# The stored sample states enter the product with q as plain float32, in four column tiles of TensorE

## The reference

```
def retention_chunk(q, k, v, S):
    ...
    scores = jnp.einsum('bhld,bhmd->bhlm', q, k) * dmask
    out = (jnp.einsum('bhlm,bhmv->bhlv', scores, v)
           + jnp.einsum('bhld,bhdv->bhlv', q, S) * q_decay[:, :, None])
    S_new = S * s_decay[:, None, None] + jnp.einsum('bhmd,bhmv->bhdv', k * k_decay[:, :, None], v)
    return out, S_new
```

## Time and profile before

| | |
|---|---|
| median of 3 runs | 1718.25 us (1717.4 to 1718.27) |
| the profiled execution | 1717.73 us |
| its span, first to last instruction | 1716.2 us |
| PE busy | 1691.2 us (99%) |
| DVE busy | 1109.4 us (65%) |
| ACT busy | 670.4 us (39%) |
| mean granted TensorE clock | 0.997 of 2.4 GHz |

### The profile page before, as it was taken

The page is one execution under the profiler, slowest core; times in us unless marked ns, Lnnn a source line. Parts: engine busy times, 40 slices in busy tenths (PEclk is TensorE's granted clock), DMA queues, the critical chain, the costliest instruction groups (busy, mean ns, idle before and its releaser), DMA issues.

```text
span 1716.2 us, 30964 instructions
## 1 busy us (share of the span) xinstructions
PE 1691.2 (99%) x11054; PEld 1642.6 (96%) x11054; DVE 1109.4 (65%) x1700; ACT 670.4 (39%) x982; POOL 172.1 (10%) x239
## 2 busy tenths in 40 slices
PE   7999999999999999999999999999999999999996
PEld 7999999999999999999999999999999999999995
DVE  6656657656656665765675665787776666666465
ACT  4533433443343343343243334453333333333333
POOL 1000000100100100000010010340000000000243
PEclk9999999999999999999999999999999999999998
DMA  8547846865764774784785586444754444444442
GB/s 329 183 149 250 286 149 226 299 185 172 283 234 155 280 270 155 258 280 137 259 292 169 184 287 217 142 138 139 243 197 147 147 147 147 147 147 150 148 147 98
DMA packets 101657, 342.04 MB, mean 199 GB/s; under 512 B 13680, under 2 KB 18416, under 8 KB 101568
## 3 DMA queue, kind: packets, MB, share of 16 engines
q1 hardware_dynamic: 81216, 265.49, 46.2%
q0 software_dynamic: 20352, 75.24, 12.9%
HBM read 292.30 MB, written 40.52 MB: 194 GB/s over the span
## 4 chain that ended last, share of the span: by engine, by line
PE 97%; ACT 1%; DVE 1%; DMA 0%; SPq 0%; issue 0%; POOL 0%; ACTq 0%; DVEq 0%; POOLq 0%
PE proj L1274 24%; PE proj L1279 24%; PE proj L1275 24%; PE proj L1420 4%; PE proj L1428 4%; PE proj L1421 4%; PE qs L1384 2%; PE qs L1385 2%; PE side L1265 1%; PE side L1260 1%; PE side L1259 1%; PE side L1258 1%; PE side L1296 1%; PE qs L1258 0%; PE qs L1259 0%; PE qs L1260 0%
## 5 line engine op out<-in xcount | busy, mean ns | idle before, releaser
L1274 PE MATMUL proj<-x_hi,w_hi 128*128 128x322 f32 (+2 forms) x2528 | 768.0, 314 | 8.2 <-DVE x_lo L796 7.9
L1275 PE MATMUL proj<-x_lo,w_hi 128*128 128x322 f32 (+2 forms) x2528 | 764.5, 313 | 0.0
L526 ACT CAST w_hi<-w_raw 128x1024 fp32r<-128x1024 f32 x416 | 435.6, 1049 | 429.7 <-PE proj L1275 238.9
L786 DVE TENSOR_TENSOR w_lo<-w_raw,w_hi 128x1024 fp32r<-128x1024 f32 x416 | 513.6, 1238 | 82.8 <-ACT w_hi L526 61.3
L1274 PEld LDWEIGHTS proj<-x_hi,w_hi 128*128 128x128 f32 x2528 | 477.8, 189 | 18.2 <-issue 12.2
L1275 PEld LDWEIGHTS proj<-x_lo,w_hi 128*128 128x128 f32 x2528 | 477.1, 189 | 4.2
L1279 PE MATMUL proj<-x_hi,w_lo 128*128 128x322 f32 (+2 forms) x2528 | 431.3, 313 | 0.7 <-DVE w_lo L786 0.7
L1279 PEld LDWEIGHTS proj<-x_hi,w_lo 128*128 128x128 f32 x2528 | 391.8, 189 | 1.2 <-DVE w_lo L786 1.2
L1420 PE MATMUL proj<-qk_or_z,w_hi 128*128 128x322 f32 x480 | 146.3, 315 | 0.2
L1421 PE MATMUL proj<-qk_or_z,w_hi 128*128 128x322 f32 x480 | 144.0, 311 | 0.0
L877 DVE TENSOR_TENSOR s_lo<-te_for_q_or_prompt_state,s_hi 128x512 fp32r<-128x512 f32 x128 | 85.9, 688 | 85.7 <-ACT s_hi L563 85.6
(11 more groups left out here) (190 smaller groups left out, 1442.7 us busy)
## 6 DMA issues: line engine op xcount, KB each, us to landing
w_raw<-w_head SPq DMA_DIRECT2D x256, 512.0 KB, 4.2
w_raw<-w_conv SPq DMA_DIRECT2D x128, 512.0 KB, 3.5
state_update<-s_in POOLq DMA_DIRECT2D x64, 512.0 KB, 7.3
te_for_q_or_prompt_state<-s_in SPq DMA_DIRECT2D x64, 512.0 KB, 5.2
s_out<-state_update POOLq DMA_DIRECT2D x64, 512.0 KB, 5.5
w_raw<-w_cout SPq DMA_DIRECT2D x32, 512.0 KB, 3.6
s_prompt<-te_for_q_or_prompt_state POOLq DMA_DIRECT2D x8, 512.0 KB, 3.6
head_table<-tables POOLq DMA_DIRECT2D x8, 441.0 KB, 5.0
```

Source lines behind the costliest of these rows:

```text
L526: act.copy(w_hi[:, i % SPL, :], w_raw[:, i % RAW, :]).then_inc(w_h.sem, 1)
L786: TT(w_lo[:, i % SPL, :], w_raw[:, i % RAW, :], f(w_hi[:, i % SPL, :]), ALU.subtract).then_inc(w_l.sem, 1)
L1274: mm(bank[:, 0:n], wh[:, k, :], rhs_h(k), start=(first and k == 0), stop=False)
L1275: x = mm(bank[:, 0:n], wh[:, k, :], rhs_l(k), start=False, stop=False)
```

## The change

- A state is no longer split. TensorE reads it from `sa` as plain float32, and q, multiplied with its decay by VectorE, stands in `qz` as plain float32 too.
- A matmul now has 32 stationary columns: 8 of them hold q of one sample, 24 are zero. It writes 32 partitions of the bank, which are one column tile of the array. Samples of even number and the key halves 0 and 1 take the tiles at 0 and 32, samples of odd number those at 64 and 96. `QP_AT` puts four groups of four such matmuls (two samples by two key halves) behind the chunks 6, 8, 12 and 15 of a head. Each is written as one matmul of 32 columns by 512.
- `s_round`, `s_rest`, their buffers and their semaphores go. So do the split of q for this product and ScalarE's copy into `qz`. VectorE writes `qz` with four small multiplications in place of one and two subtractions.
- `sa` has four buffers. The state loads stand at the chunks 5 to 8 and 11 to 14, those of the samples 4 to 7 wait for the group of the same head that frees their buffer (`state_pairs_used`), and the wait for the prompt's state moves from sample 0 to sample 3.
- The matrix of the fold has its ones in other rows; the fold is otherwise the same.

```
-QS_AT = {5: (0,), 6: (1,), 7: (2,), 10: (3, 4), 11: (5,), 12: (6, 7), 13: (8,), 14: (9, 10), 15: (11,),
-         16: (12, 13), 17: (14,), 18: (15,)}
+QP_AT = {6: 0, 8: 1, 12: 2, 15: 3}
-SA_AT = {5: 0, 7: 1, 12: 2, 14: 3, 16: 4, 17: 5, 18: 6, 20: 7}
+SA_AT = {5: 0, 6: 1, 7: 2, 8: 3, 11: 4, 12: 5, 13: 6, 14: 7}
...
-        qz = rb("q_spread", [DKB, NB * 136], F32R)
+        qz = rb("q_spread", [DKB, NB // 2 * 72])
-        sa = rb("state_for_q_or_prompt_state", [2, DKB, DV])
-        s_hi, s_lo = rb("s_hi", [2, DV], F32R), rb("s_lo", [2, DV], F32R)
+        sa = rb("state_for_q_or_prompt_state", [4, DKB, DV])
...
 (SyncE)
-                        sp.wait_ge(s_l.sem, s_l.at(h, 2 * b - 2))
-                        if b == 0:
+                        sp.wait_ge(s_q.sem, s_q.at(h, b // 2 - 1))
+                        if b == 3:
                             sp.sem_inc(passed.sem, 1)
                             sp.wait_ge(st_free.sem, st_free.at(h, 0))
-                        sp.dma_start(sa[:, b % 2, :, :], s_in[b, h]).then_inc(sa_in[b % 2].sem, 16)
+                        sp.dma_start(sa[:, b % 4, :, :], s_in[b, h]).then_inc(sa_in[b % 4].sem, 16)
...
 (ScalarE)
-                    act.copy(s_hi[:, t % 2, :], sa[:, b % 2, t % 2, :]).then_inc(s_h.sem, 1)
...
 (VectorE)
-                    TT(s_lo[:, t % 2, :], sa[:, b % 2, t % 2, :], f(s_hi[:, t % 2, :]), ALU.subtract).then_inc(s_l.sem, 1)
...
+                        for d in range(DKB):
+                            qd = by_pair(q_raw[:, d, NP_:N])
+                            for e in range(2):
+                                z = TT(qz_rows[e][:, d], qd[:, :, e], dec[:, :, e], ALU.mult)
+                        z.then_inc(qz_set.sem, 1)
...
 (TensorE)
-                        qb = qz[:, d, P * b:P * b + P]
-                        mm(bank_q[:, :], qb, s_hi[:, t % 2, :], start=(t == 0), stop=False)
-                        x = mm(bank_q[:, :], qb, s_lo[:, t % 2, :], start=False, stop=(t == 15))
+                        for e in range(2):
+                            b = 2 * q + e
+                            pe.wait_ge(sa_in[b % 4].sem, sa_in[b % 4].at(h, 16 * (b // 4 + 1)))
+                            for d in range(DKB):
+                                rows = slice(64 * e + 32 * d, 64 * e + 32 * d + 32)
+                                x = mm(bank_q[rows, :], qz[:, d, 32 * b:32 * b + 32], sa[:, b % 4, d, :],
+                                       start=(q == 0), stop=(q == NB // 2 - 1))
                         x.then_inc(s_q.sem, 1)
```

More of the change, by code:

```diff
@@ L192, in hybrid_step @@
         y_n = vt_yn[:, :].rearrange("p (t n) -> p t n", t=3)
-        pst = sa[:, 0]
-        qz_rows = qz[:, :, :].rearrange("p k (b c) -> p k b c", c=136)
+        pst = sa[:, 3]
+        qz_rows = [qz[:, :, :].rearrange("p k (q c) -> p k q c", c=72)[:, :, :, 32 * e:32 * e + DSEQ] for e in range(2)]
         ret.close()
@@ L230, in hybrid_step @@
         q_t, q_rot, q_h, q_l = count("q_temp"), count("q_rotated", 2), count("q_hi_made"), count("q_lo_made")
-        qs_t, qz_h, qz_l = count("q_decayed"), count("q_spread_hi"), count("q_spread_lo")
+        qz_set = count("q_spread_set")
         k_t, k_rot, k_h, k_l = count("k_temp"), count("k_rotated", 2), count("k_hi_made"), count("k_lo_made")
@@ L239, in hybrid_step @@
         vt_done, vn_h, vn_l = count("v_turned", 3), count("v_rows_hi", 3), count("v_rows_lo", 3)
[L240 to L243, removed]
+        sa_in = [count(f"state_q_in{i}", 32) for i in range(4)]
+        s_q = count("state_pairs_used", NB // 2, 1)
         yf_h, yf_l = count("y_fold_hi"), count("y_fold_lo")
@@ L384, in _ @@
             pool.memzero(a_lo[:, :].bitcast(F32))
-            pool.memzero(qz[:, :, :].bitcast(F32))
+            pool.memzero(qz[:, :, :])
             pool.memzero(k_ps[:, :].bitcast(F32))
@@ L578, in side @@
                         act.copy(q_hi, q_raw).then_inc(q_h.sem, 1)
[L579 to L582, removed]
                     if i == 8:
@@ L616, in side @@
                     if i == 19:
-                        act.wait_ge(s_q.sem, s_q.at(h, 2 * NB))
+                        act.wait_ge(s_q.sem, s_q.at(h, NB // 2))
                         act.copy(y_f[:, 0, :], bank_q[:, :]).then_inc(yf_h.sem, 1)
@@ L636, in head @@
                     side(i)
-                    for t in QS_AT.get(i, ()):
-                        s_round(t)
                     if last and i == 25:
@@ L789, in _ @@
             dve.sem_inc(p_dve.sem, p_dve.credit)
-            dve.sem_inc(s_l.sem, s_l.credit)
             dve.sem_inc(s_new.sem, s_new.credit)
@@ L898, in side @@
                         dve.wait_ge(q_rot.sem, q_rot.at(h, 2))
-                        dec = tab[:, QD_AT:QD_AT + NSAMP].unsqueeze(1).to_broadcast([P, DKB, NSAMP])
-                        qs = tmp[:, 0, 0:DKB * NSAMP].rearrange("p (d n) -> p d n", d=DKB)
-                        TT(qs, q_raw[:, :, NP_:N], dec, ALU.mult).then_inc(qs_t.sem, 1)
+                        by_pair = lambda ap: ap.rearrange("p (q e r) -> p q e r", e=2, r=DSEQ)
+                        dec = by_pair(tab[:, QD_AT:QD_AT + NSAMP])
+                        for d in range(DKB):
[3 more added lines that the diff above has]
+                        z.then_inc(qz_set.sem, 1)
                         dve.wait_ge(q_h.sem, q_h.at(h))
                         TT(q_lo, q_raw, f(q_hi), ALU.subtract).then_inc(q_l.sem, 1)
[L904 to L908, removed]
                     if i == 6:
@@ L994, in head @@
                         side(i)
-                    for t in QS_AT.get(i, ()):
-                        s_rest(t)
                     for back, t in due(KU_AT, i, first, last):
@@ L1374, in side @@
                         mm(bank_q[:, :], k_ps[:, c], v_ps[:, :], start=False, stop=True).then_inc(st_done.sem, 1)
[L1375 to L1381, removed]
-                            pe.wait_ge(st_read.sem, st_read.at(h, 0))
-                        qb = qz[:, d, P * b:P * b + P]
-                        mm(bank_q[:, :], qb, s_hi[:, t % 2, :], start=(t == 0), stop=False)
-                        x = mm(bank_q[:, :], qb, s_lo[:, t % 2, :], start=False, stop=(t == 15))
+                    if i in QP_AT:
+                        q = QP_AT[i]
+                        if q == 0:
+                            pe.wait_ge(qz_set.sem, qz_set.at(h))
+                            pe.wait_ge(st_read.sem, st_read.at(h, 0))
+                        for e in range(2):
[5 more added lines that the diff above has]
+                                       start=(q == 0), stop=(q == NB // 2 - 1))
                         x.then_inc(s_q.sem, 1)
@@ L1611, in head_tables @@
     for j in range(NSAMP):
-        con[[j, NSAMP + j], 2 * P + META + j] = 1.0
+        b, r = j // DSEQ, j % DSEQ
+        for d in range(DKB):
+            con[64 * (b % 2) + 32 * d + DSEQ * (b // 2) + r, 2 * P + META + j] = 1.0
     return tables, trig, con
```

## The result

Median of 4 runs 1695.47 us (1695.32 to 1695.75) against 1718.22 us before (1717.4 to 1718.27); ratio 0.9869, 95% interval 0.9857 to 0.9881. The forecast was 1739 us, slower. The profiled execution took 1695.32 us, its span 1693.7 us.

The account below looks back on a forecast made before the run. TensorE, busy for 1691.2 of 1716.2 us, was taken as the bound. From 1717.73 us, 60.2 us of removed matmuls went off and 81.3 us of new groups came on: 1738.8, forecast 1739 us, range 1693 to 1752 us.

Parts of the forecast that it names:

- The bound, and the exchange rate: In the heads TensorE is always busy, so each microsecond it gains or loses is one of the whole.
- What goes, 60.2 us: TensorE loses 256 split float32r matmuls of 512 columns, 0.235 us each: 60.2 us saved.
- The price of one plain float32 product: Each written plain float32 matmul of 512 columns becomes two records of 0.43 us on TensorE, 0.86 us together.
- The way in and out: Entering and leaving tiles costs TensorE 0.39 us a group beside its stream, taken from the state update's row tiles.
- How the four overlap: A group's four column tiles overlap neighbours by half, in program order: five record times, 2.54 us a group, 81.3 us in all.
- full overlap: Rival: all four column tiles of a group run together, 1.25 us a group, 1697.5 us in all; chance 0.33.
- the sign of being wrong that the prediction named: Starts of a group's matmuls within some nanoseconds of one another, or TensorE waiting for state_q_in or w_hi behind chunk 12.
- The chance: Chances given to the cases of overlap in a group; by sign faster 0.36, the same 0.05, slower 0.59.
- The rest of the edit at nothing: ScalarE's 77.0 us and VectorE's 85.9 us of removed splits, the q_spread multiplications and the fold count as nothing under TensorE.
- SyncE's queue: State loads waiting for buffers at two places a head cost nothing; at most 67 us if their cover were gone.
- The second wait: SyncE stands at chunk 13 from about 43 us until the second group ends at 49.4 us; next load some 3 us late.

Follow-up runs that it names:

- one tile: The changed kernel with each group's four matmuls put into one and the same column tile, otherwise the same work: 1777.08 us, 1.0341 of the kernel before.
- plain: The changed kernel with plain float32 states but no column tiles, 16 matmuls a head with 128 stationary columns: 1768.88 us, 1.0297 of the kernel before.
- two tiles: The changed kernel with eight places a head, two matmuls each in two column tiles: 1731.89 us, 1.0079 of the kernel before.
- two places: The changed kernel with two groups of eight matmuls a head instead of four of four: 1691.87 us tile by tile, 1691.61 us by sample pairs.
- with the work put back: The changed kernel plus the removed roundings (ScalarE) and subtractions (VectorE), on other data, TensorE not waiting for them: 1697.96 us, 0.9884 of the kernel before.

## Why the prediction was wrong, point by point

- **The bound, and the exchange rate.** Right. TensorE is busy for the whole stretch of the heads after too, and each microsecond of its stream was one of the whole.
- **What goes, 60.2 us.** Right within what the sum can tell: counted from the kernel before, the sums of five kernels with this term (changed, one tile, plain, two tiles, two places) come within 3 us of their times.
- **The price of one plain float32 product, two records of 0.43 us.** Right: eight in a row in one tile last 3.62 us, 8 x 0.43 and a latency.
- **The way in and out.** 0.35 us for 0.39. Right, except that 0.19 us of it are saved where row tiles stand beside it.
- **How the four overlap.** This step failed. I wrote "If TensorE starts matmuls in program order, tile 1's first record starts only with tile 0's second", and took it because "nothing in the trace shows a matmul that overtakes another". Nothing in that trace could have shown it: its only tiles have one record each. (The LayerNorm rows show one record after the other within the whole array, and say nothing of two tiles.) The group measured 1.20 us against 2.54: all four tiles ran together, and the second record of each held back only its own tile. That is 43 us over 32 groups, and this alone turned the sign. The mechanism that I described exists, but its steps overlap by four records; a group of the change has two records a tile and never comes to it. The rule of the Trainium skill that I leaned on ("TensorE: Matmul & The Clock Gate", Part 3: matmuls start strictly in program order) does not hold between column tiles here: written tile by tile, sixteen records took 1.94 us, which needs tile 1 to start ahead of tile 0's second to fourth record. The same part's span model, one matmul's time and about 4 ns for each further tile, led to the 1.25 us of full overlap, against 1.20 us measured; the first records of the group's four tiles start 6 to 7 ns apart, which is the sign of being wrong that the prediction named.
- **The chance.** Full overlap stood at 0.33 with 1697.5 us, 2 us from the median. The range began at 1693 us and holds the time; sign and forecast did not.
- **The rest of the edit at nothing.** Right as a term of this sum, which closes within 0.7 us without it. What the forecast didn't see is that the relief was needed on the faster side: with the work put back, TensorE loses some 2.6 us to waits for VectorE.
- **SyncE's queue.** Right that it costs nothing, half right in how. One wait a head is there, at the fifth state load: in the first head it is issued at 38.67 us, when the first group ends, and the load of chunk 12 at 39.05 us, as before. The second wait, forecast until 49.4 us at chunk 13, doesn't come: the second group started at 46.16 us and SyncE reached the load at 47.70 us. So there are 8 waits in place of 16, at most 2.3 us long (what SyncE waited for: us, times, longest). The state loads take longer to land than in the earlier trace rows, and no wait of TensorE for them shows:

```profile
SPq L355 <- PE qs L1357: 11.7, 8, 2.3
```

```profile
te_for_q_or_prompt_state<-s_in SPq DMA_DIRECT2D x64, 512.0 KB, 9.7
```

## What to carry to other kernels

Where a stationary operand has few columns, four column tiles can pay for plain float32's slower records: here four products in 1.20 us, where eight split float32r matmuls took 1.88. Write the matmuls round the tiles, with as many tiles in work at once as there are, and collect them at few places, since a group pays 0.35 us for the way into its tiles and out. And when the sign hangs on a step that no row of the trace can show, the chances should say so: here "Nothing in the trace shows" it was an absence of rows, not a row.

## What the runs showed of the hardware that was not expected

- A column tile behaves as if it had a queue of its own. Up to four records (two plain float32 matmuls) of one tile can be under way or wait while the next tile, written later, starts: 4 records a tile gave 1.94 us for sixteen, 6 a tile 5.43 us for 24, 16 a tile 22.59 us for 64. Whether row tiles do the same, and whether operands with one record a matmul can wait four deep, was not tried.
- A plain float32 record that streams 512 columns takes 0.43 us with 32 stationary columns and with 128 alike (3.62 and 3.60 us for eight).
- Four tiles that all read the same 128 partitions don't slow each other: 64 records in four tiles last 7.07 us, 16 record times and a latency.
